# Query and key transposes of a latent-attention layer moved from TensorE to transposing DMAs

## The chip, the cores and the metric

The kernel runs on one core of a Trainium2 chip. The metric is the device time of one execution in microseconds: the median of the runs shown. An engine's work is told by the names of the profile: PE is TensorE, PEld its weight load, DVE VectorE, ACT ScalarE, POOL GpSimd and SP SyncE, which here issues DMAs alone.

## What is computed

Two decoder layers over 512 tokens of width 1024: multi-head latent attention (MLA), then sparse attention (NSA). The change touches only the first:

```python
def mla_mixer(h, pos, w_in, g_cq, w_uq, g_ckv, w_ukv, g_q, g_k, w_out):
    c_q, c_kv, k_pe, z = jnp.split(h @ w_in, [384, 640, 704], axis=-1)
    q = (rms_norm(c_q, g_cq) @ w_uq).reshape(B, S, 16, 192)
    kv = (rms_norm(c_kv, g_ckv) @ w_ukv).reshape(B, S, 16, 128 + 128)
    k_nope, v = kv[..., :128], kv[..., 128:]
    k = jnp.concatenate([broadcast(k_pe), k_nope], axis=-1)      # 64 + 128
    q = rope(rms_norm(q, g_q), pos, 64)
    k = rope(rms_norm(k, g_k), pos, 64)
    o = causal_block_attention(q, k, v, 192 ** -0.5)             # softmax(q k^T) v
    return (o.reshape(B, S, 2048) * silu(z)) @ w_out
```

The inputs are float32. Matmuls that need the precision are made of high and low pieces: a = a_hi + a_lo, and a product is hi x hi + hi x lo + lo x hi (helper `mm3`, lines 97 to 99).

## The kernel before

The attention of layer 0 is a hand-written pipeline over `SLOTS0` = 64 slots: 16 heads times 4 tiles of 128 tokens (slot s is head s // 4, tile i = s % 4). No planner orders it: each engine has a function `step(s)` that writes its instructions of slot s in the order in which they stand, and semaphores tie the engines together. An engine runs its own list strictly in that order. Before slot 0 stand eight slots (`KV0` = -8) with only the early steps.

On PE a slot s is, in order: `scores(s)`, five fp16 matmuls of one query tile with the (i + 1) x 128 keys up to it (lines 97 to 99, 1249, 1250); `turn(s + 4)`; `project_kv(s + 8)`, six matmuls of 256 columns; in slots with i = 1 `values` of the head before (line 1280, eight matmul records); `turn_probs(s - 1)`, transposes of the softmax weights (1263) and of a part of the gate (1270); in even slots `project_q`, nine matmuls of 384 columns, for one tile of a pair of heads.

`turn(m)` (lines 1231, 1232) makes four float32 transposes of 128 x 128 by matmuls with the identity: the 128 plain columns and the doubled 64 rotated columns of the query tile `qn` and of the key tile `kn`, four slots before their scores, into one of two PSUM banks `x_bank` (banks 6 and 7). ACT's `high(m)` (line 1659) rounds the bank to fp16 into `qkT_hi`; DVE's `low(m)` (2300, 2302, 2304) subtracts that from the bank and writes the low pieces.

What comes before `turn`: ACT's `q_stats` (1638) and `kv_stats` (1649, 1653) take sums of squares, and copy keys and values from PSUM to `kv_sb`; POOL's `q_factor` (1966, 1967) and `k_factors_of` (1974 to 1978) make the norm's factors and the rotated key columns; DVE's `scale_q` (2266) and `scale_k` (2291) scale; POOL's `rotate` (1994 to 1997) turns the rotary columns of the query. What comes after: DVE's `maximum(s)` (2313) masks the scores and takes the maximum, ACT's `exponential(s)` (1667) makes the weights, PE's `turn_probs(s)` turns them in the next slot, and ACT's `probs_out` (1674; DVE's 2320 for i = 2) copies them out for `values`. DVE's `gate` (2332) multiplies a finished head with its gate.

Weights of a head (256 KB for keys and values, 576 KB for a pair's queries) come by DMAs from SP's queue (`load_kv` 1010, `load_q` 1001); ACT splits them (1630, 1622), DVE subtracts (2259, 2254). `project_q` has one bank from tile 4 on (bank 4) and waits until the tile before is scaled; `project_kv` has one from tile 8 on (bank 5) and waits until the tile before is copied out.

## Time and profile before

| | us |
|---|---|
| median of 3 runs | 869.14 (868.8 to 869.91) |
| the profiled execution, its time | 868.95 |
| its span | 867.2 |
| PE busy in the span | 848.3 |
| DVE, ACT, POOL busy | 562.8, 502.0, 485.5 |
| layer 0's attention, scores of slot 0 to scores of slot 63 | 146.9 to 362.6 |

The span is the time between the first and the last record of the profile; 1.75 us of the execution lie around it. Busy time of an engine is the union of its instructions; a matmul's duration overlaps the next one's, so what a matmul costs is the distance from its start to the next start.

### The profile page before, as it was taken

To read this page: it belongs to the slowest core of one execution; us is meant where nothing else is said; L and a number is where in the kernel's file an instruction comes from. 1 tells how busy PE (TensorE), PEld (TensorE's weight loads), DVE (VectorE), ACT (ScalarE), POOL (GpSimd) and SP (SyncE) were. 2 spreads that over 40 slices of the span, in tenths; PEclk is the share of its full clock that TensorE was granted. 3 is DMA by queue.
4 is the path that set the end of the run, shared out by engine and by line. 5 is a ranking of instruction groups with operands and counts; after the bars stand their busy time and mean duration, and the time that the engine had idled before them with its cause. 6 is when DMAs were issued, how large, how long until landed. Compare 5 with 4: busy or idle time off the path is not lost.

```text
span 867.2 us, 16773 instructions
## 1 busy us (share of the span) xinstructions
PE 848.3 (98%) x6041; PEld 709.4 (82%) x6041; DVE 562.8 (65%) x1607; ACT 502.0 (58%) x1151; POOL 485.5 (56%) x627
## 2 busy tenths in 40 slices
PE   6999999999999999999999999999999999999998
PEld 6999998888888888778888888778887677777786
DVE  5899988887878787653111113278689688888521
ACT  6456667887877778652134223434443789898610
POOL 2000407876767686343347424366675699999731
PEclk9999999999999999999999999999999999999999
DMA  6433322111111101122227222222233100100011
GB/s 217 131 98 98 98 79 77 39 52 51 43 28 37 53 14 50 49 97 97 96 93 134 93 92 65 80 97 74 79 97 97 50 3 2 51 3 2 2 49 49
DMA packets 39324, 58.93 MB, mean 68 GB/s; under 512 B 8757, under 2 KB 22346, under 8 KB 39242
## 3 DMA queue, kind: packets, MB, share of 16 engines
q1 hardware_dynamic: 39200, 57.85, 21.4%
q8 instruction: 49, 0.80, 0.4%
q14 instruction: 33, 0.27, 0.1%
q10 hardware_dynamic: 42, 0.01, 0.0%
HBM read 55.63 MB, written 2.10 MB: 67 GB/s over the span
## 4 chain that ended last, share of the span: by engine, by line
PE 85%; DVE 8%; ACT 3%; issue 2%; POOL 1%; DMA 0%; ACTq 0%; DVEq 0%; POOLq 0%
PE bank L97 19%; PE bank L99 18%; PE bank L98 18%; PE bank L1280 4%; DVE w_lo L2180 2%; PE bank L502 2%; PE bank L484 2%; PE bank L1263 2%; PE bank L511 2%; PE bank L503 2%; PE bank L1231 1%; PE bank L1232 1%; PE bank L591 1%; PE bank L592 1%; PE bank L590 1%
## 5 line engine op out<-in xcount | busy, mean ns | idle before, releaser
L2003 POOL TENSOR_TENSOR w_lo<-w_raw,w_hi 128x2048 fp32r<-128x2048 f32 (+1 forms) x26 | 118.4, 4554 | 124.0 <-ACT w_hi L1728 123.9
L97 PE MATMUL bank<-w_hi,h_hi 128*128 128x512 f32 (+3 forms) x472 | 171.4, 363 | 1.7 <-DVE h_lo L2100 1.0
L99 PE MATMUL bank<-w_hi,h_lo 128*128 128x512 f32 (+3 forms) x472 | 166.8, 353 | 0.0
L98 PE MATMUL bank<-w_lo,h_hi 128*128 128x512 f32 (+3 forms) x472 | 166.8, 353 | 0.0
L1728 ACT ACTIVATE w_hi<-w_raw 128x2048 fp32r<-128x2048 f32 (+1 forms) x26 | 49.2, 1893 | 94.0 <-PE bank L99 94.0
L97 PEld LDWEIGHTS bank<-w_hi,h_hi 128*128 128x128 f32 x472 | 88.7, 188 | 15.1 <-issue 3.4
L99 PEld LDWEIGHTS bank<-w_hi,h_lo 128*128 128x128 f32 x472 | 88.7, 188 | 11.5
L98 PEld LDWEIGHTS bank<-w_lo,h_hi 128*128 128x128 f32 x472 | 88.9, 188 | 10.1
L789 POOL TENSOR_TENSOR p<-kvr,p 128x512 f16<-128x512 f32 (+1 forms) x96 | 88.5, 942 | 10.1 <-ACT p L705 9.9
L97 PE MATMUL bank<-w_hi,o_hi 128*128 128x512 f32 x192 | 77.2, 402 | 0.8 <-DVE o_lo L2340 0.8
L99 PE MATMUL bank<-w_hi,o_lo 128*128 128x512 f32 x192 | 75.8, 395 | 0.0
L98 PE MATMUL bank<-w_lo,o_hi 128*128 128x512 f32 x192 | 75.8, 395 | 0.0
L97 PE MATMUL bank<-w_hi,c_hi 128*128 128x256 f32 (+1 forms) x224 | 75.6, 337 | 0.0
L98 PE MATMUL bank<-w_lo,c_hi 128*128 128x256 f32 (+1 forms) x224 | 68.3, 305 | 0.0
L99 PE MATMUL bank<-w_hi,c_lo 128*128 128x256 f32 (+1 forms) x224 | 68.3, 305 | 0.0
L702 ACT ACTIVATE kvr<-bank,g_cols 128x512 f32<-128x512 f32 (+1 forms) x96 | 60.6, 632 | 7.5 <-PE bank L518 7.5
L839 DVE CUSTOM_DVE_ANT_0 scored<-bank,band 128x128 f32<-128x128 f32 (+3 forms) x128 | 56.1, 483 | 10.3 <-PE bank L484 10.3
L705 ACT ACTIVATE p<-bank,g_cols 128x512 f16<-128x512 f32 (+1 forms) x96 | 60.8, 633 | 0.0
L2313 DVE CUSTOM_DVE_ANT_0 below<-bank,band,g_cols 128x128 f32<-128x128 f32 (+1 forms) x64 | 34.4, 538 | 23.3 <-PE bank L1250 23.0
L1659 ACT ACTIVATE qkT_hi<-bank 128x512 f16<-128x512 f32 x64 | 38.3, 598 | 12.6 <-PE bank L1232 12.5
L97 PEld LDWEIGHTS bank<-w_hi,o_hi 128*128 128x128 f32 x192 | 36.1, 188 | 9.1 <-POOL w_lo L2003 1.0
L97 PEld LDWEIGHTS bank<-w_hi,c_hi 128*128 128x128 f32 x224 | 42.2, 188 | 1.3
(367 smaller groups left out, 2440.9 us busy)
## 6 DMA issues: line engine op xcount, KB each, us to landing
w_raw<-in_nsa_w_in SPq DMA_DIRECT2D x10, 1024.0 KB, 5.0
w_raw<-in_mla_w_in SPq DMA_DIRECT2D x8, 1024.0 KB, 5.2
w_raw<-in_mla_w_out SPq DMA_DIRECT2D x8, 1024.0 KB, 5.0
w_raw<-in_nsa_w_in SPq DMA_DIRECT2D x8, 984.0 KB, 5.0
w_raw<-in_nsa_w_out SPq DMA_DIRECT2D x4, 1024.0 KB, 5.1
w_raw<-in_mla_w_uq SPq DMA_DIRECT2D x7, 576.0 KB, 4.2
w_raw<-in_mla_w_ukv SPq DMA_DIRECT2D x15, 256.0 KB, 2.7
w_raw<-in_mla_w_in SPq DMA_DIRECT2D x4, 704.0 KB, 5.7
```

Source lines behind the costliest of these rows:

```text
L97: nc.tensor.matmul(out, a[0], b[0], start=start, stop=False)
L98: nc.tensor.matmul(out, a[0], b[1], start=False, stop=False)
L99: return nc.tensor.matmul(out, a[1], b[0], start=False, stop=stop)
L702: nc.scalar.activation(p32(k, u), src, ACT.Exp, scale=score_scale[:, 0:1])
L705: nc.scalar.activation(piece_of(p1, n, u), src, ACT.Exp, scale=score_scale[:, 0:1]).then_inc(exp_done, 1)
L789: nc.gpsimd.tensor_tensor(piece_of(p2, n, u), p32(k, u), piece_of(p1, n, u), ALU.subtract).then_inc(sub_done, 1)
L839: last = nc.vector.tensor_tensor_reduce(scored[k % 2][:, w * keys:(w + 1) * keys], first_bank(k)[:, w * keys:(w + 1) * keys], band[:, SEQ ...
L1280: last = nc.tensor.matmul(o_bank[:, j * P:SEQ], kv_sb[:, h % 4 * NT + j, NOPE:WKV], probT[h % 2][:, j * ROW + j * P:j * ROW + SEQ], start= ...
L1659: nc.scalar.activation(qkT_hi[m // NT % 2][:, :, t * P:(t + 1) * P], x_bank[m % 2][:, :].rearrange("p (a t) -> p a t", a=4), ACT.Copy).the ...
L1728: nc.scalar.activation(w_hi[g % 2][:, :, 0:width], w_raw[g % 2][:, :, 0:width], ACT.Copy).then_inc(m_hi, 1)
L2003: nc.gpsimd.tensor_tensor(w_lo[g % 2][:, :, 0:width], w_raw[g % 2][:, :, 0:width], w_hi[g % 2][:, :, 0:width].bitcast(F32), ALU.subtract). ...
L2313: nc.vector.tensor_tensor_reduce(below[i % 2][:, 0:keys], score_bank[i % 2][:, 0:keys], band[:, SEQ - keys:SEQ], score_scale[:, 1:2], -LEA ...
```

## The change

The turned query and key pieces no longer come from PE. They are made before they are turned, in fp16 in SBUF, and a DMA turns them:

- `turn` on PE, `high` on ACT, `low` and `scale_k` on DVE and the two banks `x_bank` go. The key's gain is multiplied into the query's gain once, so keys need no gain of their own.
- ACT's `key_high(m)` rounds a key tile to fp16 straight from `kv_sb`, three slots behind its projection, and `query_high(m)` a query tile of two heads from `qn`, four slots behind. DVE's `key_low` and `query_low` make the low pieces in the same slots. A key tile then is 4 blocks of 128 fp16 columns (`k16`, three pairs of tiles), a query tile of one head 3 blocks (`q16`, six tiles of two heads).
- SP's new `turn(m)` issues two transposing DMAs from SBUF to SBUF, 3 blocks (96 KB) and 4 blocks (128 KB), into `qkT`. It waits until tile m - 2 has landed whole, so that at most two tiles are in flight, and until the scores of the head two before are done. PE's `scores(s)` waits until both have landed. 64 tiles make 128 such DMAs, 14 MB.
- Weight loads stand among them in SP's queue, four slots earlier in its list than their split. `mid_piece(1)` (1 MB for the next stage) moves from behind the loop to slot 52 of it.
- The freed banks go to the projections: from tile 4 and 8 on `project_q` and `project_kv` alternate between two banks each, and wait for the tile before the last instead of the last.
- POOL writes the rotated columns once, not doubled, and its `k_factors_of(m)` waits until the pair of tiles six and five before has landed.

```diff
+Q32, Q16, KPAIRS = 3, 6, 3
...
+        LATENT_GAINS = SPARSE_GAINS + 1
...
+                k16 = [place(f"k16_{b}", (22, 24, 31)[b] * KB, [P, 2, KCOLS], F16) for b in range(KPAIRS)]
+                qn = place("qn", 26 * KB, [P, Q32, 2, QK])
...
-                qkT_hi = [place(f"qkT_hi{a}", (54 + 8 * a) * KB, [P, 4, SEQ], F16) for a in range(2)]
-                qkT_lo = [place(f"qkT_lo{a}", (70 - 4 * a) * KB, [P, 3, SEQ], F16) for a in range(2)]
-                kn = place("kn", 86 * KB, [P, QRING, WIDE])
+                qkT = [place(f"qkT{a}", (54 + 7 * a) * KB, [P, 7, SEQ], F16) for a in range(2)]
+                q16 = place("q16", 83 * KB, [P, Q16, 2, QCOLS], F16)
                 rot = place("rotq", 92 * KB, [P, 4, 2, HALF0])
...
-                x_bank = [bank[6], bank[7]]
...
-                SLOTS0, KV0, T0 = H * NT, -8, -4
+                SLOTS0, KV0, AHEAD = H * NT, -8, 3
...
-                q_of = lambda m: bank[(4, 0, 3, 2)[m]] if m < NT else bank[4]
-                kv_of = lambda m: bank[1] if m < 2 * NT and m % 2 else bank[5]
+                q_of = lambda m: bank[(4, 0, 3, 2)[m]] if m < NT else bank[4 + m % 2 * 3]
+                kv_of = lambda m: bank[1] if m < 2 * NT and m % 2 else bank[5 + m % 2]
...
-                x_tile = lambda s: s - T0 if 0 <= s - T0 < SLOTS0 else None
+                k_split, q_split = (lambda s: k_tile(s - 3)), (lambda s: q_tile(s - 4))
...
+                all_landed = lambda eng, m: eng.wait_ge(x_landed[m % 2], 32 * (m // 2 + 1))
...
+                    def turn(m):
+
+                        n, t = m // NT, m % NT
+                        mq, tok = n // 2 * NT + t, slice(t * P, (t + 1) * P)
+                        if m >= 2:
+                            all_landed(sp, m - 2)
+                        if n >= 2:
+                            sp.wait_ge(s_done, NT * (n - 1))
+                        sp.wait_ge(x_lo, q_pieces[mq])
+                        sp.dma_start_transpose(qkT[n % 2][:, 0:3, tok], q16[:, mq % Q16, n % 2, :]).then_inc(x_landed[m % 2], 16)
+                        sp.wait_ge(x_lo, k_pieces[m])
+                        sp.dma_start_transpose(qkT[n % 2][:, 3:7, tok], k16_of(m)).then_inc(x_landed[m % 2], 16)
+
...
+                        if s == SLOTS0 - 12:
+                            mid_piece(1)
+                        if 0 <= s + AHEAD < SLOTS0:
+                            turn(s + AHEAD)
+                        if (k_weights(s + 4) or 0) > 1:
+                            load_kv(k_weights(s + 4))
+                        if (q_weights(s + 4) or 0) > 1:
+                            load_q(q_weights(s + 4))
...
-                        if m > NT:
-                            pe.wait_ge(q_scaled, m)
+                        if m == NT + 1:
+                            pe.wait_ge(z_sum, Z_STEPS * NZ)
+                        if m > NT + 1:
+                            pe.wait_ge(q_scaled, m - 1)
...
-                        if 2 <= m <= 2 * NT:
+                        if m >= 2:
                             pe.wait_ge(kv_out, m - 1)
-                        if m > 2 * NT:
-                            pe.wait_ge(kv_out, m)
...
-                    def turn(m):
...
-                        dst = x_bank[m % 2]
-                        q, k = qn[:, mq % QRING, n % 2, :], kn[:, m % QRING, :]
-                        for part, src in enumerate((q, k)):
-                            nc.tensor.transpose(dst[:, 2 * part * P:(2 * part + 1) * P], src[:, 2 * ROPE:WIDE], ident[:, :])
-                            last = nc.tensor.transpose(dst[:, (2 * part + 1) * P:(2 * part + 2) * P],
-                                                       src[:, 0:2 * ROPE], ident[:, :])
-                        last.then_inc(x_done, 1)
...
-                        pe.wait_ge(x_free, s + 1)
+                        all_landed(pe, s)
...
-                        if x_tile(s) is not None:
-                            turn(x_tile(s))
...
-                            act.wait_ge(k_scaled, m - NT + 1)
+                            act.wait_ge(x_lo, k_pieces[m - NT])
...
-                    def high(m):
-                        act.wait_ge(x_done, m + 1)
-                        t = m % NT
-                        nc.scalar.activation(qkT_hi[m // NT % 2][:, :, t * P:(t + 1) * P],
-                                             x_bank[m % 2][:, :].rearrange("p (a t) -> p a t", a=4),
-                                             ACT.Copy).then_inc(x_hi, 1)
+                    def key_high(m):
+
+                        act.wait_ge(kv_out, m + 1)
+                        act.wait_ge(k_rotated, m // 2 + 1)
+                        nc.scalar.activation(k16_of(m)[:, 0:NOPE], kv_sb[:, m % (4 * NT), 0:NOPE], ACT.Copy,
+                                             scale=ms_k[:, m % NT:m % NT + 1]).then_inc(x_hi, 1)
+
+                    def query_high(m):
+
+                        act.wait_ge(q_rotated, m + 1)
+                        if m >= Q16:
+                            all_landed(act, (m - Q16) // NT * 2 * NT + NT + (m - Q16) % NT)
+                        nc.scalar.activation(q16[:, m % Q16, :, ROPE:ROPE + QK], qn[:, m % Q32, :, :], ACT.Copy).then_inc(x_hi, 1)
...
+                        if k_split(s) is not None:
+                            key_high(k_split(s))
+                        if q_split(s) is not None:
+                            query_high(q_split(s))
...
-                        if x_tile(s) is not None:
-                            high(x_tile(s))
...
+                        if m >= 2 * KPAIRS:
+                            all_landed(pool, m - 2 * KPAIRS)
+                            all_landed(pool, m - 2 * KPAIRS + 1)
+                        nc.gpsimd.tensor_tensor(k16[m // 2 % KPAIRS][:, :, 2 * P:3 * P].rearrange("p m (c d) -> p m c d", c=2),
...
+                        nc.gpsimd.tensor_tensor(q[:, :, 0:HALF0], rot[:, 0], rot[:, 3], ALU.subtract)
+                        nc.gpsimd.tensor_tensor(q[:, :, HALF0:ROPE], rot[:, 1], rot[:, 2], ALU.add).then_inc(q_rotated, 1)
...
+                        if m >= Q32:
+                            dve.wait_ge(x_lo, q_pieces[m - Q32])
...
+                    def key_low(m):
+
+                        dve.wait_ge(x_hi, k_pieces[m])
+                        k, factor = k16_of(m), ms_k[:, m % NT:m % NT + 1]
+                        nc.vector.scalar_tensor_tensor(k[:, NOPE:2 * NOPE], kv_sb[:, m % (4 * NT), 0:NOPE], factor,
+                                                       k[:, 0:NOPE], ALU.mult, ALU.subtract)
+                        nc.vector.scalar_tensor_tensor(k[:, KCOLS - ROPE:KCOLS], kpe_sb[:, m % NT, :], factor,
+                                                       k[:, 2 * P:2 * P + ROPE], ALU.mult, ALU.subtract).then_inc(x_lo, 1)
+
+                    def query_low(m):
+
+                        dve.wait_ge(x_hi, q_pieces[m])
+                        q, whole_q = q16[:, m % Q16, :, :], qn[:, m % Q32, :, :]
+                        nc.vector.tensor_tensor(q[:, :, 2 * P:3 * P], whole_q[:, :, ROPE:QK], q[:, :, P:2 * P], ALU.subtract)
+                        nc.vector.tensor_tensor(q[:, :, 0:ROPE], whole_q[:, :, 0:ROPE], q[:, :, ROPE:P],
+                                                ALU.subtract).then_inc(x_lo, 1)
...
+                            og.link(nc.vector.tensor_tensor(gq0[:, ROPE:QK], gq0[:, ROPE:QK], gk0[:, ROPE:QK], ALU.mult))
```

How PE's list changes, in slot 3 of head 0 (i = 3): the last two of the scores, then what follows. Before:

```order
L1249 MATMUL bank<-qkT_hi_99 128x512
L1250 MATMUL bank<-qkT_lo_101,qkT_hi_99 128x512
L1231 MATMUL bank<-ident,qn 128x128
L1232 MATMUL bank<-ident,qn 128x128
L1231 MATMUL bank<-ident,kn 128x128
L1232 MATMUL bank<-ident,kn 128x128
L97 MATMUL bank<-w_hi,c_hi 128x256
L98 MATMUL bank<-w_lo,c_hi 128x256
L99 MATMUL bank<-w_hi,c_lo 128x256
```

Now:

```order
L1255 MATMUL bank<-qkT_102 128x512
L1256 MATMUL bank<-qkT_102 128x512
L97 MATMUL bank<-w_hi,c_hi 128x256
L98 MATMUL bank<-w_lo,c_hi 128x256
L99 MATMUL bank<-w_hi,c_lo 128x256
```

The four transposes are gone and the projection stands right behind the scores. The same goes in all 64 places where `turn` stood, slots -4 to 59.

ACT's list, from the exponential of slot 2 (384 keys) through that of slot 3 (512 keys). Before:

```order
L1667 ACTIVATE prob,rowsum<-below_106,negmax 128x384
L1638 ACTIVATE sq_junk,ms_q<-bank 128x192 x2
L1659 ACTIVATE qkT_hi_100<-bank 128x4x128
L1649 ACTIVATE sq_junk,ms_k<-bank 128x128
L1653 ACTIVATE kv_sb<-bank,ms_c 128x256
L1667 ACTIVATE prob,rowsum<-below_107,negmax 128x512
L1659 ACTIVATE qkT_hi_99<-bank 128x4x128
```

Now (`k_1_72` is a `k16`, `q_104` is `q16`):

```order
L1678 ACTIVATE prob,rowsum<-below_107,negmax 128x384
L1664 ACTIVATE k_1_72<-kv_sb,ms_k 128x128
L1642 ACTIVATE sq_junk,ms_q<-bank 128x192 x2
L1653 ACTIVATE sq_junk,ms_k<-bank 128x128
L1657 ACTIVATE kv_sb<-bank,ms_c 128x256
L1678 ACTIVATE prob,rowsum<-below_108,negmax 128x512
L1664 ACTIVATE k_1_72<-kv_sb,ms_k 128x128
L1672 ACTIVATE q_104<-qn 128x2x192
```

The rounding of the turned bank stood between `q_stats` and `kv_stats`, behind PE's transposes; now a smaller one of the keys stands at the slot's start, in even slots followed by that of the queries.

SP's list around one load of a pair's query weights. Before there was nothing but loads (three here, two of them the same); now:

```order
L1074 DMA_TRANSPOSE qkT_102<-q_104 128x3x128
L1076 DMA_TRANSPOSE qkT_102<-k_1_72 128x4x128
L1009 DMA w_raw<-in_mla_w_uq 128x3x384
L1074 DMA_TRANSPOSE qkT_103<-q_104 128x3x128
L1076 DMA_TRANSPOSE qkT_103<-k_2_73 128x4x128
L1074 DMA_TRANSPOSE qkT_103<-q_104 128x3x128
L1076 DMA_TRANSPOSE qkT_103<-k_2_73 128x4x128
L1018 DMA w_raw<-in_mla_w_ukv 128x2x256
```

Between two weight loads now lie two or four tiles, each with two transposing DMAs that wait for pieces of their slots.

## Rows read from the trace of the kernel before

**Rows 1.** The page, part 1: busy time of each engine
```profile
PE 848.3 (98%) x6041; PEld 709.4 (82%) x6041; DVE 562.8 (65%) x1607; ACT 502.0 (58%) x1151; POOL 485.5 (56%) x627
```

**Rows 2.** The page, part 4: shares of the chain that ended last
```profile
PE 85%; DVE 8%; ACT 3%; issue 2%; POOL 1%; DMA 0%; ACTq 0%; DVEq 0%; POOLq 0%
```

**Rows 3.** Busy us by stretch: total, then PE, PEld, DVE, ACT, POOL, PEclk, DMA, GB/s
```profile
157.44:341.78 184.34, 184.34 (x1292) 157.36 (x1292) 146.20 (x460) 144.22 (x496) 136.61 (x288) 1.00 0.13 40
139.87:157.44 17.57, 15.52 (x116) 14.20 (x115) 14.43 (x48) 15.38 (x53) 14.00 (x31) 1.00 0.16 49
```

**Rows 4.** Timeline, PE: start us, us, engine, line, operation, out<-in, count
```profile
244.33 0.27 PE L1231 MATMUL bank<-ident,qn 128*128 128x128 f32 x1
...
244.69 0.37 PE L97 MATMUL bank<-w_hi,c_hi 128*128 128x256 f32 x1
...
246.09 0.28 PE L1231 MATMUL bank<-ident,qn 128*128 128x128 f32 x1
246.20 0.27 PE L1232 MATMUL bank<-ident,qn 128*128 128x128 f32 x1
...
246.42 0.27 PE L1232 MATMUL bank<-ident,kn 128*128 128x128 f32 x1
246.56 0.36 PE L97 MATMUL bank<-w_hi,c_hi 128*128 128x256 f32 x1
...
247.35 0.60 PE L1263 MATMUL bank<-ident,prob 128*128 128x128 f32 x4
```

**Rows 5.** Timeline, ACT, the same two slots
```profile
245.68 0.28 ACT L1649 ACTIVATE sq_junk<-bank 128x128 f32<-128x128 f32 x1
...
246.31 0.72 ACT L1667 ACTIVATE prob<-below,negmax 128x512 f32<-128x512 f32 x1
246.92 0.20 ACT L1667 ACTIVATION_READ_ACCUMULATOR prob<-below,negmax 128x1 f32 x1
```

**Rows 6.** Groups by line and shape, 157.44 to 341.78 us: busy us, mean ns
```profile
L1659 ACT ACTIVATE qkT_hi<-bank 128x512 f16<-128x512 f32 x52 | 31.2, 599 | 11.4 <-PE bank L1232 11.3
...
L2291 DVE SCALAR_TENSOR_TENSOR kn<-kv_sb,ms_k,gk 128x128 f32<-128x128 f32 x52 | 23.3, 449 | 0.0
...
L2300 DVE TENSOR_TENSOR qkT_lo<-bank,qkT_hi 128x256 f16<-128x256 f32 x52 | 21.6, 415 | 0.5 <-ACT qkT_hi L1659 0.5
...
L2302 DVE TENSOR_TENSOR qkT_hi<-bank,qkT_hi 64x128 f16<-64x128 f32 x52 | 15.3, 294 | 0.7
...
L2304 DVE TENSOR_TENSOR qkT_lo<-bank,qkT_hi 64x128 f16<-64x128 f32 x52 | 14.7, 282 | 0.7
...
L1685 ACT ACTIVATE zT<-bank 128x256 f32<-128x256 f32 x25 | 9.7, 386 | 0.1
...
L1674 ACT ACTIVATE probT<-bank 128x128 f32<-128x128 f32 x13 | 3.6, 278 | 22.7 <-PE bank L1270 22.7
```

**Rows 7.** DMA issues: line, queue, count, KB each, us to landing
```profile
w_raw<-in_mla_w_ukv SPq DMA_DIRECT2D x15, 256.0 KB, 2.7
...
v_diag<-vcmp SPq DMA_DIRECT2D x4, 32.0 KB, 4.1
```

**Rows 8.** Timeline, SP: four issues of 32 KB
```profile
604.35 2.64 SPq L1079 DMA_DIRECT2D v_diag<-vcmp  x4
```

**Rows 9.** Timeline, PE, the first slots: two waits on the subtraction
```profile
143.03 0.30 PE L1231 MATMUL bank<-ident,qn 128*128 128x128 f32 x1 [0.70 <-DVE qkT_lo L2304]
...
148.74 0.30 PE L1231 MATMUL bank<-ident,qn 128*128 128x128 f32 x1 [1.35 <-DVE qkT_lo L2304]
```

**Rows 10.** Timeline, POOL, the first slots
```profile
143.62 0.50 POOL L1994 TENSOR_TENSOR rotq<-qn,tcos 128x128 f32<-128x128 f32 x1 [1.70 <-DVE qn L2266]
...
146.90 0.61 POOL L1978 TENSOR_TENSOR kn<-kpe_sb,ms_k 128x256 f32<-128x256 f32 x1
```

**Rows 11.** Timeline, PE, slot 56: its wait on the exponential
```profile
345.69 0.66 PE L1263 MATMUL bank<-ident,prob 128*128 128x128 f32 x4 [0.48 <-ACT prob L1667]
```

More of the change, by code:

```diff
@@ L2347, in step @@
                             z_sums(NB - 1)
[L2348 to L2349 removed]
+                        if k_split(s) is not None:
+                            key_low(k_split(s))
                         if 1 <= s <= SLOTS0 and s % NT == 3:
                             probs_out(s - 1)
[L2352 to L2353 removed]
+                        if q_split(s) is not None:
+                            query_low(q_split(s))
                         if q_tile(s - 1) is not None:
```

107 lines of the change are left out of this document (36 added, 71 removed).

## The prediction

> **What bounds the kernel now.** I read the page's first part before anything else: PE is busy 848.3 of 867.2 us [rows 1], and it holds 85% of the chain that ended last [rows 2]. So a change of PE's list moves the end, and one of another engine does so only where PE comes to wait for it. Then busy time by stretch. From 157.44 us (the scores of slot 3) to 341.78 us (those of slot 55) lie 13 groups of four slots, and PE is busy in all of the 184.34 us at a granted clock of 1.00 [rows 3]: 14.18 us a group, 3.545 us a slot. The others are busy in that stretch, over 13: DVE 11.2, ACT 11.1, POOL 10.5 us a group. There the whole of what PE sheds is gain, until one of them ends later than PE. In the first slots (139.87 to 157.44) PE is busy 15.52 of 17.57 us, so about 2 us of waits lie there.
>
> The timeline of PE shows one seam closely [rows 4]. `turn` takes 0.44 us: its four transposes start 0.11 apart, from 246.09 to 246.42, so it ends at 246.53.  The 273 ns of one transpose overlap the next and are not the price.
>
> **What PE sheds.** 64 x 0.44 = 28.2 us. That is the upper bound of the gain of this part, and 52 of the 64 lie in the steady stretch, 4 x 0.44 = 1.76 us a group.
>
> **What comes to be late next.** The walk through one group [rows 4, 5] looks for the wait that takes the place. Of PE's waits on ACT the closest is `turn_probs` of i = 3. The last projection of slot 3 starts at 244.69; ACT's `kv_stats` begins when it is through, at 245.68, the exponential of 512 keys begins at 246.31 and its read ends at 247.12. Its transposes start on PE at 247.35. So 0.23 us stand between the two. In that interval PE loses just one `turn`, that of slot 0 (the one of slot 3 lies ahead of the projection and shifts both). PE then is ready at 247.35 - 0.44 = 246.91, and ACT, which still begins `kv_stats` behind the same projection, at 247.12 plus some 0.05: PE waits 0.26, say 0.29 us. That is once a group. In the other three slots PE has a query projection or `values` between the turns of the weights; the same walk leaves some 0.3 us to spare for i = 1, and more for the rest. Two-bank projections cost nothing and give nothing here: PE has no wait on a projection's bank in the steady stretch, and none can be won. They are needed as PE comes sooner, and they hide ACT's copies.
>
> Steady stretch: 13 x (1.76 - 0.29) = 19.1 us; a slot then takes 12.71 / 4 = 3.18 us.
>
> **The other engines.** ACT loses 4 x 0.60 and gains four key roundings of 128 columns and two query roundings of 384 columns a group. Nearest rows: 0.28 for 128 columns, 0.39 for 256, 0.60 for 512 [rows 6], so 4 x 0.28 + 2 x 0.49 = 2.1, and ACT stands at 10.8 of 12.7 us. None of the new ones waits for PE: their slot is three or four behind. DVE loses 4 x (0.45 + 0.42 + 0.29 + 0.28) = 5.8 us and gains 4 x (0.45 + 0.29) + 2 x (0.42 + 0.29) = 4.4 [rows 6]: 9.8 us. POOL writes half as much in two of a rotation's four instructions and stays under its 10.5. All three fit into 12.7, so I cost them at nothing beyond the 0.29. If that cover is gone (an engine at 100%), each microsecond of its group is paid 13 times.
>
> **The transposing DMAs.** The trace has none, and this is the open price. Per tile there are two, of 96 and 128 KB. From below: a plain load of 256 KB lands 2.7 us after its issue; from above: a copy from SBUF to SBUF of 32 KB lands in 4.1 us [rows 7]. SP needs 2.64 us for four such issues [rows 8], 0.66 each, so its queue can issue a tile in 1.3 us if a transposing issue costs no more. Two bounds count. Rate: a tile must pass in 3.18 us. At 2.7 us each DMA it passes in 2.7 if a tile's two run one behind the other and two tiles overlap, in 1.4 if all four overlap. Delay: the tightest tile is i = 3 of an even head. Its query pieces are made in slot 4n and its scores stand three slots later, 9.5 us; by the walk the pieces are through some 3.5 us into the slot, so 6 us remain. Two DMAs one behind the other at 2.7 land in 5.4. I take both as hidden, by the row nearer in size; at 4.1 each, 8.2 us, they would be about 2 us late once in eight slots.
>
> Here one page of the Trainium skill speaks against the change and one for it. By the Trainium skill, VectorE: DVE Perf Modes, "The three transpose paths", a DMA transpose of 128x128 bf16 takes 1309 ns, against 390 ns on TensorE; if that held per block, seven blocks made 9.2 us a tile, an estimate, and the sum would turn from -21 to some +340 us. By the Trainium skill, Advanced Engine Details and Errata, "X-Bar Transpose (TRN2)", transposing DMAs are about as fast as plain ones (350-400 GB/s); 224 KB would then pass in some 0.6 us, an estimate, and the sum stays. No row here shows either.
>
> **The two ends.** First slots: eight turns, 3.5 us, and two waits of PE on the subtraction for the bank, 0.70 and 1.35 us [rows 9], could all go: 5.5 us at most. But POOL is the slow one there: a rotation and a pair of key factors run from 143.62 to 147.51 [rows 10], and now ACT, in its own order, cannot pass the key rounding that needs them. Walking the lists, the first turned weights come some 3 us sooner and those of slot 1 only 2. At least nothing; I take 2.0. Last slots: slot 56 waits 0.48 us for its exponential already [rows 11], so the turns of slots 56 to 59 were free, and I count 0.4 for slot 55's. `mid_piece(1)` in another place is not waited for and costs nothing.
>
> **The sum.** 19.1 + 2.0 + 0.4 = 21.5 us. The profiled execution took 868.95 us (its span 867.2), so 847.4; the median stands 0.2 above that, and I predict **847.6 us**.
>
> **Rivals.**
> First, the other sign: **the transposing DMAs pass more slowly than the slots**. One mechanism: SP waits until tile m - 2 has landed, PE until its own has, and from then on a slot lasts as long as a tile's two DMAs. It decides from 3.18 us a tile on; from 3.545 us on the change loses. Over 60 slots: at 4.1 us a tile, (4.1 - 3.545) x 60 = +33, about 902; at 2.7 us for each of the two with no overlap, 5.4: +111, about 980; at 4.1 each, 8.2: +279, about 1148. For it: the copy that stays in SBUF is the slow row, 4.1 us for an eighth of the bytes [rows 7], and a queue that serves turned blocks one at a time fits both ends. Against it: the DMA engines' share is 0.13 in the stretch [rows 3], and that copy touches 32 partitions. The 1309 ns of the Trainium skill, told above, would be this rival at its far end. 0.25.
> Second, **the pieces come late, not slowly**: landings of 6 to 8 us from the piece, or POOL and ACT held in their queues by the new waits on landings, so that PE waits 0.3 to 1.2 us more a group: 13 x 0.3 to 13 x 1.2, 4 to 16 us given back, 852 to 864. POOL has 2.2 us a group to spare, and DVE now has two SBUF sources in more of its instructions. 0.14.
> Third, **the gain is eaten whole**: the weights' loads stand behind waiting turns and come late, or the waits above sum to 20 us; within 0.2% of before. 0.04.
> Fourth, above my forecast: the wait of 0.29 does not come and the first slots give all: 28 us, about 841. It is inside the forecast's own spread.
>
> **The numbers.** Forecast 0.57, its own range 841 to 852. All that I call unknown is the DMA, so the chances follow from it. Faster by over 0.2% (about what a measurement of this kernel can tell from no change): 0.57 + 0.14 = 0.71. Same 0.04. Slower 0.25, of which about a quarter lies below 885 us. The range is 842 to 885: it leaves out some 0.01 below and 0.19 above.
>
> **What would show it.** In the profile after: no matmul from `ident` and `qn` or `kn`, and the projection 0.22 us behind the last start of the scores; a group of four slots of 12.7 us; before `turn_probs` of i = 3 a wait of about 0.3 us on ACT's exponential, 14 or so times; ACT over 80% busy there; no wait of PE on the first score matmul. A transposing DMA landing in 2 to 3 us and SP waiting for pieces, not for landings. The prediction is wrong if the score matmuls wait for DMAs in every slot (the first rival: then a slot's length is that of two landings), or if they wait once in eight slots (the second).

## The result and the profile after

The changed kernel takes **854.76 us** (median of 4 runs, 853.98 to 856.51), the kernel before beside it 869.52: a ratio of 0.9833, 95% interval 0.9814 to 0.9852. That is 14.8 us faster, where I had forecast 21.5: outside the forecast's own 841 to 852 us, inside the range of 842 to 885. The profiled execution took 855.4 us, its span 853.6. Of the four executions two, this one and that of 856.51 us, have a mean granted clock of TensorE of 0.994, and two (854.13 and 853.98 us) one of 0.998.

The page of the changed kernel, part 1 and the shares of the chain that ended last:

```profile
PE 827.9 (97%) x5785; PEld 686.6 (80%) x5785; DVE 552.8 (65%) x1544; ACT 493.1 (58%) x1183; POOL 484.2 (57%) x628
...
PE 79%; DVE 9%; ACT 5%; issue 3%; DMA 2%; SPq 1%; POOL 1%; ACTq 0%; DVEq 0%; POOLq 0%
```

PE lost 20.4 us of busy time against [rows 1], the span only 13.6: about 7 us became idle time of PE, and its share of the chain fell from 85% to 79% [rows 2]. To see where, I cut both spans at the same five instructions: the first matmul of the query projection of tile 3 (slot -5, the second projection behind the z products), the first score matmul of slots 3, 55 and 63, and the end.

| stretch | before, us | after, us | difference | forecast |
|---|---|---|---|---|
| start to tile 3's query projection | 138.29 | 139.50 | +1.21 | 0 |
| to the scores of slot 3 | 19.15 | 19.54 | +0.39 | -2.0 |
| to the scores of slot 55 (13 groups) | 184.34 | 166.26 | -18.08 | -19.1 |
| to the scores of slot 63 | 20.81 | 23.78 | +2.97 | -0.4 |
| to the end of the span | 504.61 | 504.52 | -0.09 | 0 |
| sum | 867.2 | 853.6 | -13.60 | -21.5 |

The steady stretch did what it should. Most of what is missing lies in its two ends. Busy us of the changed kernel in the three middle stretches (total, then PE, PEld, DVE, ACT, POOL, granted clock, DMA share, GB/s), to be read beside [rows 3] and beside the same two end stretches of the kernel before, which come first:

```profile
138.29:157.44 19.15, 17.09 (x126) 15.75 (x125) 15.98 (x52) 16.12 (x56) 14.78 (x33) 1.00 0.14 45
341.78:362.59 20.81, 19.38 (x124) 14.42 (x122) 15.75 (x52) 15.89 (x42) 9.11 (x10) 1.00 0.15 52
```
```profile
139.50:159.04 19.54, 16.77 (x98) 15.07 (x97) 15.25 (x49) 16.23 (x60) 14.03 (x33) 0.83 0.42 94
159.04:325.30 166.26, 163.81 (x1084) 135.93 (x1084) 135.33 (x407) 136.82 (x522) 134.68 (x284) 1.00 0.57 117
325.30:349.08 23.78, 19.30 (x104) 13.16 (x102) 17.51 (x44) 14.78 (x42) 11.03 (x14) 0.93 0.47 107
```

The granted clock was 1.00 in all of this before; now it is 0.83 and 0.93 in the ends. PE is idle in them for 2.77 and 4.48 us (before 2.06 and 1.43). In the steady stretch, DVE, ACT and POOL are busy for 81 to 82% (10.4, 10.5, 10.4 us a group of 12.8).

**The steady stretch.** The seam that [rows 4] and [rows 5] showed before, on PE and on ACT of the changed kernel (timeline: start us, us, engine, line, operation):

```profile
201.09 0.28 PE L99 MATMUL bank<-w_hi,c_lo 128*128 128x256 f32 x1
201.51 0.65 PE L1269 MATMUL bank<-ident,prob 128*128 128x128 f32 x4
```
```profile
200.02 0.28 ACT L1653 ACTIVATE sq_junk<-bank 128x128 f32<-128x128 f32 x1 [0.43 <-PE bank L99]
...
200.29 0.47 ACT L1657 ACTIVATE kv_sb<-bank,ms_c 128x256 f32<-128x256 f32 x1
200.65 0.72 ACT L1678 ACTIVATE prob<-below,negmax 128x512 f32<-128x512 f32 x1
201.26 0.20 ACT L1678 ACTIVATION_READ_ACCUMULATOR prob<-below,negmax 128x1 f32 x1
```

Products of 256 columns start 0.12 us apart, so PE would have begun the turn of the weights at 201.21; it began at 201.51, 0.05 behind the exponential's read. This is the wait of 0.29 us once a group. PEld's group of the same line has idled 3.8 us for the exponential, 0.29 on the mean of the 13 groups (the waits stand in 11 of them, at most 0.4 each):

```profile
L1269 PEld LDWEIGHTS bank<-ident,prob 128*128 128x128 f32 x130 | 15.1, 140 | 3.8 <-ACT prob L1678 3.8
L97 PE MATMUL bank<-qkT 128*128 128x512 f16 (+3 forms) x52 | 15.9, 305 | 0.9 <-DMA qkT<-k 0.9
```

The second row is the other loss: PE waits twice for a landing, together 0.9 us, at 187.63 and 265.04. A group of four slots took 14.30 us before and takes 12.87 now, two of them 13.23 and 13.04. The last of the 13 has less work in either kernel: 12.71 us before, 11.28 now.

**The transposing DMAs.** SyncE's timeline, and the view of all instructions on `qkT` (duration in ns, min/median/max, then the time from issue to landing):

```profile
204.28 1.18 SPq L1074 DMA_TRANSPOSE qkT<-q  x1
205.50 1.26 SPq L1076 DMA_TRANSPOSE qkT<-k  x1
206.81 0.58 SPq L1009 DMA_DIRECT2D w_raw<-in_mla_w_uq  x1
```
```profile
L1074 SPq DMA_TRANSPOSE qkT<-q x64: 1177/1190/2217, 143.9 to 342.3; - x64
L1076 SPq DMA_TRANSPOSE qkT<-k x64: 1249/1264/2268, 145.2 to 343.6; - x64
...
DMA to landing us min/median/max: 2.3/2.5/5.6
```

They land in 2.5 us in the median, the queries' 96 KB and the keys' 128 KB alike, near the 2.7 us that I took. But an issue takes 1.19 and 1.26 us of SP's queue, where I had 0.66: 2.5 us of each slot's 3.2, and a weight load more in some slots. From one tile's first issue to the next tile's it is 2.6 us where SP waits for nothing. By the Trainium skill, VectorE: DVE Perf Modes, "The three transpose paths", a 128x128 block takes 1309 ns; three blocks and four land in the same median of 2.5 us here, so that figure does not add up by blocks. By Advanced Engine Details and Errata of the Trainium skill, "X-Bar Transpose (TRN2)", transposing DMAs run at about the speed of plain ones; the trace agrees (a plain load of 256 KB lands in 2.9 us), but the time to issue does not follow from it.

**The first slots.** PE ends the last projection ahead of slot 0 at 146.05 and then stands. Its timeline, and busy us by stretch (columns as above):

```profile
148.49 0.29 PE L97 MATMUL bank<-qkT 128*128 128x128 f16 x1 [2.44 <-DMA qkT<-k]
```
```profile
146.00:148.50 2.50, 0.06 (x2) 0.01 (x1) 1.67 (x6) 2.19 (x8) 2.19 (x6) 0.89 0.46 95
148.50:151.00 2.50, 2.28 (x12) 2.02 (x13) 1.93 (x5) 2.09 (x10) 0.82 (x3) 0.50 0.43 83
```

Tile 0's query pieces are through at 143.85, its DMAs are issued at 143.88 and 145.22, and the keys have landed at 148.4. The granted clock is 0.50 (1.2 of 2.4 GHz) from 147.95, still in the idle time, until 154.8. What this fall costs can be read from runs told below, whose lists are the same up to slot 3. From the scores of slot 0 to those of slot 3, in the changed kernel, in e1 and in e5 (columns as above):

```profile
148.49:159.04 10.55, 10.33 (x54) 9.03 (x55) 7.29 (x24) 7.91 (x33) 7.92 (x19) 0.70 0.63 142
```
```profile
148.31:157.79 9.48, 9.02 (x55) 8.16 (x55) 6.40 (x22) 7.79 (x33) 7.09 (x18) 0.82 0.56 120
```
```profile
148.09:157.22 9.13, 7.97 (x55) 6.77 (x55) 6.24 (x21) 7.69 (x33) 6.74 (x17) 1.00 0.54 107
```

PE idled 2.44, 2.45 and 2.51 us ahead of them, and yet the clock was at 0.50 for 6.8 us in the first, for 3.4 us in the second and not at all in the third. The long fall costs 1.4 us here against none. A mean clock of 0.998 over the run leaves room for one fall of 3.4 us alone (an estimate, 1.7 of 853.6 us, and the last slots have such a fall); so two of the four executions above probably had no long fall.

**The last slots.** Timelines of DVE, POOL and PE:

```profile
332.56 4.42 DVE L2309 SCALAR_TENSOR_TENSOR k<-kv_sb,ms_k,k 128x128 f16<-128x128 f32 x1 [1.05 <-ACT k L1664]
...
337.17 0.59 DVE L2328 CUSTOM_DVE_ANT_0 below<-bank,band,g_cols 128x384 f32<-128x384 f32 x1
```
```profile
332.31 4.52 POOL L2018 TENSOR_TENSOR w_lo<-w_raw,w_hi 128x2048 fp32r<-128x2048 f32 x1 [0.50 <-ACT w_hi L1741]
```
```profile
338.57 0.55 PE L1269 MATMUL bank<-ident,prob 128*128 128x128 f32 x3 [2.42 <-ACT prob L1678]
```

`key_low` (L2309), 0.35 us elsewhere, took 4.42 and ended 0.15 us behind POOL's first `mid_low`, a subtract of 128x2048 that begins in slot 57. The maximum of slot 58 stands behind it on DVE, ACT's exponential behind that, and PE waits 2.42 us; the clock is 0.50 from 339.1 to 342.5. In the kernel before, the same subtract (349.35, 4.54 us) met subtractions that read a bank of PSUM, and none took long. By the Trainium skill, SBUF — State Buffer, "SBUF: two separate sides", VectorE with two inputs in SBUF and GpSimd share one port pair, which the first holds for its whole instruction; the rows agree.

### The profile page after: what moved, and what is told of

Same layout as the page of the kernel before. It is cut to its first block, busy times and chain, and to the rows that moved or that the text cites. A ratio compares the mean times of both kernels' runs of the same rounds, so it can differ in the third digit from the quotient of the medians.

```text
span 853.6 us, 16381 instructions
## 1 busy us (share of the span) xinstructions
PE 827.9 (97%) x5785; PEld 686.6 (80%) x5785; DVE 552.8 (65%) x1544; ACT 493.1 (58%) x1183; POOL 484.2 (57%) x628
## 4 chain that ended last, share of the span: by engine, by line
PE 79%; DVE 9%; ACT 5%; issue 3%; DMA 2%; SPq 1%; POOL 1%; ACTq 0%; DVEq 0%; POOLq 0%
PE bank L97 18%; PE bank L99 18%; PE bank L98 18%; PE bank L1286 3%; DVE w_lo L2198 2%; PE bank L510 2%; PE bank L492 2%; PE bank L519 2%; PE bank L511 2%; PE bank L1269 1%; DMA qkT<-k 1%; PE bank L599 1%; ACT prob L1678 1%; PE bank L600 1%; PE bank L598 1%
## 5 line engine op out<-in xcount | busy, mean ns | idle before, releaser
L97 PE MATMUL bank<-w_hi,c_hi 128*128 128x256 f32 (+1 forms) x224 | 78.6, 351 | 0.3 <-DVE w_lo L2277 0.2
L98 PEld LDWEIGHTS bank<-w_lo,c_hi 128*128 128x128 f32 x224 | 43.1, 192 | 0.4
```

The source lines that it names most:

```text
L97: nc.tensor.matmul(out, a[0], b[0], start=start, stop=False)
L98: nc.tensor.matmul(out, a[0], b[1], start=False, stop=False)
```

## The experiments

Each kernel was timed beside runs of the kernel before; I compare the ratios, since those runs are not the same for all.

**e1, e2, e3: the two ends.** e1 cuts the subtract:

```diff
-    nc.gpsimd.tensor_tensor(w_lo[g % 2][:, :, 0:width], ...)
+    for k, c in parts:          # g == 0: KP x 2 parts of 128x256; else one
+        last = nc.gpsimd.tensor_tensor(w_lo[g % 2][:, ks, cs], ...)
+    last.then_inc(m_lo, 1)
```

> The changed kernel with GpSimd's first mid_low (128x2048 subtract, 4.52 us) cut into eight subtracts of 128x256, about 0.57 us each by size. Theory A (GpSimd's long subtract holds VectorE's key_low, which has two operands in SBUF, for 4.42 us in place of 0.35, and all of the tail's loss follows from that): key_low takes at most about 1 us here, the idle time of TensorE before the turned probabilities of slot 58 falls from 2.42 to under 0.5 us, the 3.4 us at a granted clock of 0.50 behind it go, the last group of slots takes 11 to 12 us in place of 14.18, and the kernel 851.5 to 852.5 us against the changed kernel's 854.8. Rival B (VectorE is held until GpSimd's whole row of subtracts is done, whatever their size): the last group stays near 14.2 us, 854.8. Rival C (the clock falls there for another reason): the wait goes, the clock still falls, some 853.

Measured: 852.26 us (852.05 to 853.73), ratio 0.9813 (0.9799 to 0.9826). By the ratios that is 1.7 us less than the changed kernel, and the two intervals overlap a little; the cleaner pair is e2 and e3 below, timed together and apart by this edit alone. The timelines of DVE and of PE in e1:

```profile
331.94 0.63 DVE L2314 SCALAR_TENSOR_TENSOR k<-kv_sb,ms_k,k 128x128 f16<-128x128 f32 x1 [1.12 <-ACT k L1664]
```
```profile
334.98 0.39 PE L97 MATMUL bank<-qkT 128*128 128x512 f16 x1 [0.96 <-DMA qkT<-k]
...
337.59 0.23 PE L97 MATMUL bank<-qkT 128*128 128x128 f16 x1 [1.02 <-DMA qkT<-k]
```

`key_low` is held for about one eighth of the subtract, 0.6 to 0.9 us; the wait for the exponential and the fall of the clock are gone, and slots 55 to 63 take 21.22 us in place of 23.78. Theory A holds and B and C fall. In place of the old wait PE now waits twice, about 1 us each, for the DMAs of slots 59 and 60: these two slots take 2.61 and 2.60 us, and SP begins a tile every 2.6 us there (333.81, 336.42, 339.02).

e2 makes the first query pieces earlier:

```diff
-k_split, q_split = (lambda s: k_tile(s - 3)), (lambda s: q_tile(s - 4))
+k_split, q_split = (lambda s: k_tile(s - 3)), (lambda s: q_tile(s - 3) if s < KV0 + 6
+                    else None if s == KV0 + 6 else q_tile(s - 4))
```

> The changed kernel with the query pieces of tiles 0 to 2 made one slot earlier (slots -5 to -3 in place of -4 to -2). Theory A (TensorE's 2.44 us of waiting before the scores of slot 0 come from tile 0's queries being made last, and the 6.8 us at a granted clock of 0.50 behind it come from that idle time): query pieces of tile 0 are ready near 140.5 instead of 143.85, the wait goes, the clock stays at 1.00, slot 3 begins 3 to 5 us earlier, and the kernel takes 850 to 852 us. Rival B (slot 3 is set by the other engines: GpSimd's factors and the weights' split are late anyway): the wait at slot 0 goes but turns up before slots 1 to 3, slot 3 begins under 1 us earlier, 854 to 855. Rival C (the transposing DMAs of tile 0 are slow for another reason, such as the weights' load beside them): the wait at slot 0 stays over 1 us.

Measured: 854.68 us (854.09 to 855.42), ratio 0.9837 (0.9824 to 0.9851): nothing won, as rival B has it. PE's waits in e2's timeline, and its stretch behind slot 0:

```profile
148.07 0.39 PE L97 MATMUL bank<-w_hi,c_hi 128*128 128x256 f32 x1 [2.21 <-DVE w_lo L2277]
151.84 0.27 PE L97 MATMUL bank<-qkT 128*128 128x256 f16 x1 [1.21 <-ACT kv_sb L1657]
153.76 0.33 PE L1269 MATMUL bank<-ident,prob 128*128 128x128 f32 x1 [0.50 <-ACT prob L1678]
156.55 0.44 PE L1269 MATMUL bank<-ident,prob 128*128 128x128 f32 x2 [0.94 <-ACT prob L1678]
```
```profile
148.50:151.00 2.50, 2.14 (x14) 1.82 (x12) 0.92 (x4) 1.36 (x7) 0.97 (x2) 1.00 0.54 144
```

The scores of slot 0 begin 6.41 us after tile 3's query projection instead of 8.99, with no wait, and the clock stays at 1.00. But PE then waits 2.21 us for the split of head 2's weights and another 2.65 us for ACT, and slot 3 begins 19.42 us after the projection against 19.54.

e3, both edits:

> Both edits of the two runs before. Theory: the two losses are 200 us apart and add up: 847 to 850 us, near the 847.6 forecast. Rival: one of them is eaten elsewhere (a wait at the end of the latent stage that takes whatever comes early), and the sum is no better than the better of the two by itself.

Measured: 852.25 us (851.95 to 852.42), ratio 0.9808 (0.9795 to 0.9822), the same as e1. The rival holds, and e2's edit is worth nothing in the time. Against e2 the subtract in eighths is worth 2.4 us, and no execution of the one reaches those of the other.

In the first slots e3's trace has the same lists as e2's, and takes 18.35 us where that took 19.42. The first step apart is GpSimd's `rotate`; e2, then e3:

```profile
144.70 1.16 POOL L2009 TENSOR_TENSOR rotq<-qn,tcos 128x128 f32<-128x128 f32 x1 [1.60 <-DVE qn L2286]
```
```profile
144.76 0.46 POOL L2009 TENSOR_TENSOR rotq<-qn,tcos 128x128 f32<-128x128 f32 x1 [1.60 <-DVE qn L2291]
```

Beside it run DVE's subtractions with two inputs in SBUF. In e2 they run on and POOL takes longer; in e3 two of them take longer (0.51 and 0.70 instead of 0.28 and 0.42 us). So e2's 19.42 is no limit. Without the edit the stretch takes 19.54 with the long fall of the clock, 18.49 with the short one (e1) and 18.20 with none (e5); with it 18.35. Where the clock holds, the other engines set slot 3 and the edit gives nothing; only against the long fall is it 1.2 us shorter.

**e4: what PE's turns are worth.** The kernel before, with `turn`'s loop run twice:

```diff
-for part, src in enumerate((q, k)):
+for part, src in ((0, q), (1, k)) * 2:
```

> The kernel before with each tile's four TensorE transposes made twice into the same bank: 0.44 us more TensorE work a tile, nothing more on any other engine. Theory (TensorE sets the slots of the kernel before, so its work counts one for one): +0.44 x 52 = 22.9 us in the steady stretch, and 24 to 28 in all: 893 to 898 us. Rival (a part of the transposes lies in time in which TensorE waits anyway, 0.1 to 0.2 us a tile): +13 to +20, 883 to 890.

Measured: 892.09 us, ratio 1.0269 (1.0255 to 1.0283), 23.2 us over the kernel before it, 0.9 below the theory's range and 2 above the rival's. The groups take 15.94 us instead of 14.30: 1.64 of the 1.76 us are passed on. So PE's work counts nearly one for one, and the first slots, where seven turns (slots -4 to 2) add 3.1 us, took only 1.4 us more (20.54 instead of 19.15).

**e5: the wait on the exponential.** On the kernel of e1:

```diff
+if 0 <= s < SLOTS0 and s % NT == 3:
+    exponential(s)
 if k_tile(s):
     kv_stats(k_tile(s))
...
-if 0 <= s < SLOTS0:
+if 0 <= s < SLOTS0 and s % NT != 3:
     exponential(s)
```

> The kernel of e1 (852.3 us) with ScalarE's exponential of every slot with i = 3 ahead of the slot's statistics of the key-value projection instead of behind them. Theory (the 0.29 us a group that I took as a new wait is real and is this: TensorE has finished the projection and waits for the exponential, which stands behind two instructions that waited for the projection): a group takes 12.57 to 12.60 in place of 12.87 us, 13 x 0.28 = 3.6 us, and the kernel 848.5 to 849.5 us. Rival (the key and value rows leave their bank 0.8 us later and something else, the next key's pieces or their transposing DMA, takes the wait over): groups of 12.8 to 13.1, no gain.

Measured: 850.51 us (849.35 to 851.47), ratio 0.9785 (0.9772 to 0.9799), 2.4 us less than e1 by the ratios and above the theory's 848.5 to 849.5. The same seam on PE and PEld's group over the stretch:

```profile
200.38 0.28 PE L99 MATMUL bank<-w_hi,c_lo 128*128 128x256 f32 x1
200.50 0.60 PE L1269 MATMUL bank<-ident,prob 128*128 128x128 f32 x4
```
```profile
L1269 PEld LDWEIGHTS bank<-ident,prob 128*128 128x128 f32 x133 | 15.6, 140 | 0.4 <-ACT prob L1678 0.4
L97 PE MATMUL bank<-qkT 128*128 128x128 f16 (+3 forms) x52 | 15.9, 306 | 3.0 <-DMA qkT<-k 3.0
```

The turn now follows 0.12 us behind the projection, and the undisturbed groups take 12.51 us, 0.36 less. But waits for landings rise to 3.0 us (1.0 in e1), and some groups take up to 13.98, so slot 3 to slot 55 is only 1.1 us shorter than in e1. The theory on the wait holds; a good part of what it gives goes to the next one, the landings.

**e6: the multiply of the gains.** The key gains are folded into the query gains by one instruction on DVE, which I had not priced. On the kernel of e1:

```diff
-        og.link(nc.vector.tensor_tensor(gq0[:, ROPE:QK], gq0[:, ROPE:QK], gk0[:, ROPE:QK], ALU.mult))
...
 split_q(1)
+og.link(nc.vector.tensor_tensor(gq0[:, ROPE:QK], gq0[:, ROPE:QK], gk0[:, ROPE:QK], ALU.mult))
 nc.vector.memset(rinv[:, :, :], 1.0).then_inc(o_free, 1)
```

> The kernel of e1 (852.3 us) with the added multiply of the query gains by the key gains (VectorE, 0.29 us at 99.47) moved out of the z products' stage to just ahead of the first slot. Theory (it lies in VectorE's chain, on which TensorE waits there; the stretch from 97 to 106 us took 8.46 us in place of 8.16): 0.3 us less, 851.9 to 852.1, which only the trace can tell. Rival (VectorE has slack there and the 0.3 us have another origin): the stretch still takes 8.46.

Measured: 851.68 us, ratio 0.9798 (0.9785 to 0.9811), not to be told from e1 by the time. The row of the changed kernel on DVE:

```profile
99.47 0.29 DVE L2398 TENSOR_TENSOR gq<-gq,gk 128x128 f32<-128x128 f32 x1
```

Between the same two products of the z stage PE takes 8.16 us before, 8.46 after the change, and 8.16 in e6. So 0.3 of the 1.21 us ahead of the slots is this instruction.

**e7: one bank each.** The changed kernel with the banks and waits of before:

```diff
-q_of = lambda m: bank[(4, 0, 3, 2)[m]] if m < NT else bank[4 + m % 2 * 3]
-kv_of = lambda m: bank[1] if m < 2 * NT and m % 2 else bank[5 + m % 2]
+q_of = lambda m: bank[(4, 0, 3, 2)[m]] if m < NT else bank[4]
+kv_of = lambda m: bank[1] if m < 2 * NT and m % 2 else bank[5]
...
-if m > NT + 1:
-    pe.wait_ge(q_scaled, m - 1)
+if m > NT:
+    pe.wait_ge(q_scaled, m)
...
-if m >= 2:
-    pe.wait_ge(kv_out, m - 1)
+if 2 <= m <= 2 * NT:
+    pe.wait_ge(kv_out, m - 1)
+if m > 2 * NT:
+    pe.wait_ge(kv_out, m)
```

> The changed kernel with one bank for the query projections and one for the key-value projections in the steady slots, as before the change, and the waits that go with it. Theory (with TensorE at 12.6 of 12.9 us a group and ScalarE emptying a bank 0.8 us after its projection, a projection finds its bank free a slot later anyway): within 1 us of 854.8, groups of 12.87. Rival (the second bank carries part of the gain, since without the turn there is 0.44 us less between a bank's last product and its next first): groups 0.3 to 1 us longer, 859 to 868.

Measured: 858.23 us (857.94 to 860.04), ratio 0.9879 (0.9866 to 0.9893), 4.0 us more than the changed kernel by the ratios, between the theory and the rival. What PE waited for from 145 to 350 us (line, releaser, total, times, longest):

```profile
PE bank L97 <- DMA qkT<-k: 3.9, 4, 2.4
PE bank L97 <- ACT kv_sb L1659: 3.7, 12, 0.3
PE bank L1271 <- ACT prob L1680: 3.5, 3, 2.3
PE bank L97 <- DVE qn L2288: 1.9, 1, 1.9
```

A new wait of 0.3 us comes once a group, but the group grows by only 0.12 us (12.99), as it covers part of the next wait: 1.6 us in 13 groups. The first slots grow by 2.2 us (21.75 instead of 19.54), where a query projection waits 1.9 us for its bank, and the last ones by 0.9, where the clock is at 0.50 for 6.9 us in place of 3.4. The second banks carry about 4 us of the gain, part of it through the clock. My "give nothing" holds only for the kernel before; "needed as PE comes sooner" is what the run shows.

**e8: the margin of the DMAs.** One tile in flight:

```diff
-if m >= 2:
-    all_landed(sp, m - 2)
+if m >= 1:
+    all_landed(sp, m - 1)
```

> The changed kernel with SyncE waiting for the landing of tile m - 1 instead of m - 2 before it issues tile m: one tile's two transposing DMAs in flight. Theory (a tile's period is then two issues of 1.2 and 1.26 us and the landing of the second, 2.5 us after its issue began, so about 3.8 us, and 5.0 if the 2.5 count from its end): TensorE waits for landings in every slot, groups of 15.2 to 20 us, the kernel 880 to 950: the rival of my prediction that the DMAs pass slower than the slots, and its deciding point of 3.2 us. Rival (landings overlap the next tile's issue even so): under 860.

Measured: 904.33 us, ratio 1.0404 (1.039 to 1.0418). SyncE's timeline in e8, and PE's waits from 150 to 400 us:

```profile
215.31 1.19 SPq L1074 DMA_TRANSPOSE qkT<-q  x1
216.54 1.26 SPq L1076 DMA_TRANSPOSE qkT<-k  x1
219.04 1.18 SPq L1074 DMA_TRANSPOSE qkT<-q  x1
```
```profile
PE bank L97 <- DMA qkT<-k: 45.9, 39, 2.9
```

A tile's period is 3.73 us, one issue and one landing, and the groups take 15.1 to 16.8. This is the first rival of the prediction, made real: at 3.73 us a tile, 0.2 over its second bound of 3.545, the kernel loses 35 us to the one before. Its point of decision was right; the formula (60 x the excess, 11 us) was too low. The 52 steady slots took 4.00 us each, not 3.73, 23.6 us in all over the kernel before: SP also issues the weights' loads in this queue, and some issues took up to 2.4 us. Another 9.9 us came in the last eight slots, which took 2.6 us each before. What keeps the change on the good side is that the next tile's issues overlap the landings.

**e9, e10, e11, e12: what is left.** e9 puts the edits of e1, e2, e5 and e6 together.

> The four edits together: GpSimd's subtract in eighths (e1), the exponential first where i = 3 (e5), the multiply of the gains moved (e6), the first three tiles' query pieces a slot earlier (e2). Theory (e5 showed that SyncE's queue with two issues of 1.2 and 1.26 us a tile, and the landings behind it, is what ends waits now, so that an earlier slot 3 and shorter groups are given back there): 849.5 to 850.5 us, with TensorE's waits for landings at the slots near 187, 212 and 288 us again. Rival (the gains add up: 0.3 for the multiply, 0.4 for the earlier start): 849.0 to 849.5.

Measured: 850.33 us (849.13 to 851.58), ratio 0.9785 (0.9773 to 0.9798), as e5 and in the theory's range. The waits for landings are there again. SP's timeline behind a load of 576 KB, and PE's:

```profile
180.25 0.57 SPq L1009 DMA_DIRECT2D w_raw<-in_mla_w_uq  x1
180.95 3.11 SPq L1074 DMA_TRANSPOSE qkT<-q  x1
```
```profile
187.26 0.23 PE L97 MATMUL bank<-qkT 128*128 128x128 f16 x1 [1.75 <-DMA qkT<-k]
```

e10 cuts this load in thirds (`part` is a third), one a slot; e11 issues each of them two slots earlier:

```diff
-if (q_weights(s + 4) or 0) > 1:
-    load_q(q_weights(s + 4))
+for part in range(KQ):
+    if (q_weights(s + 6 - part) or 0) > 1:        # e10: s + 4 - part
+        load_q(q_weights(s + 6 - part), part)
```

> The kernel of e9 with each load of query weights for a pair of heads (576 KB, one in eight slots, directly ahead of a tile's transposing DMAs) cut into three loads of 192 KB, one in each of three slots. Theory (in e5 TensorE's waits for landings, 0.25 to 1.31 us, stand at 160, 187, 212 and 288 us, each behind such a load, on whose packets the transposing DMAs wait in the 16 engines): those waits shrink to under 0.3 us, 1.5 to 2 us less than e9. Rival (it is SyncE's time to issue, which three loads of 0.5 us only lengthen): the same as e9 or up to 2 us slower.

Measured: 863.03 us (860.08 to 864.77), ratio 0.9932 (0.9917 to 0.9946). PE has no wait for a landing in the steady stretch but one of 0.5 us at its end; ACT, however, has one for the last third, which is issued two slots later than the whole load was, and all that stands behind it on ACT waits too. ACT's timeline:

```profile
191.77 1.16 ACT L1628 ACTIVATE w_hi<-w_raw 128x1152 fp32r<-128x1152 f32 x1 [2.32 <-DMA w_raw<-in_mla_w_uq]
```

Behind it comes the copy of the turned weights, for which PE waits 11.4 us in five places. I had overlooked that wait; neither the theory nor the rival has it.

> The kernel of e10 with each third loaded two slots earlier, so that the last of them is issued where the whole load was in e9. In e10 TensorE's waits for landings were gone from the steady stretch, but ScalarE waited for the last third (TensorE idle 1.6 to 3.3 us at each second head behind it). Theory (landings behind the 576 KB load were the whole of what e9 loses against groups of 12.51): all groups near 12.5, 13 of them 163.5 us in place of e9's 166.9, and the kernel 846.5 to 848 us. Rival (three issues of 0.5 us more in SyncE's queue and a third's packets still ahead of a tile's make the tiles late in smaller portions): 849 to 851.

Measured: **848.11 us** (847.18 to 848.23), ratio 0.9759 (0.9746 to 0.9773), 2.3 us less than e9 and the fastest version, 0.1 over the theory's range. Of PE's groups from slot 3 to 55 none waits for a landing but the last, 0.59 us; they take 12.50 and 12.70 us in turn (one 13.21, one 13.59, the last 11.68), 164.29 us in all against 166.95 in e9. So the landings behind the large load were most of what e9 lost against 12.5 a group.

e12 changes both ends once more:

```diff
+k_splits = lambda s: 2 if s == -3 else None if s == -2 else k_weights(s)   # ACT and DVE
...
-if s == SLOTS0 - 8:
+if s == SLOTS0 - 9:
     mid_high(0)
...
-if s == SLOTS0 - 7:
-    mid_low(0)
+if s in (SLOTS0 - 8, SLOTS0 - 7, SLOTS0 - 6):
+    mid_low(0, (slice(0, 3), slice(3, 6), slice(6, 8))[s - SLOTS0 + 8])
```

> The kernel of e11 with two more edits. (1) The split of head 2's key and value weights on ScalarE and VectorE one slot earlier, at slot -3, ahead of ScalarE's 1.28 us of table load: TensorE's 2.2 us of waiting for it at 148 us goes; theory: slot 3 begins 0.5 to 1.5 us earlier, the rest comes back as waits for ScalarE and the pair's key pieces; rival: nothing, as in e2. (2) ScalarE's rounding for the output product at slot 55 instead of 56 and GpSimd's eighths over slots 56 to 58 (3, 3, 2): TensorE's 0.6 to 0.9 us of waiting for them at slot 60 goes. Together 0.5 to 2 us under e11; if both rivals hold, the same as e11.

Measured: 851.97 us (850.29 to 853.89), ratio 0.9807 (0.9793 to 0.9822), 4 us slower than e11, which neither theory had. Its ACT and PE timelines in slots 55 and 56:

```profile
325.68 1.90 ACT L1746 ACTIVATE w_hi<-w_raw 128x2048 fp32r<-128x2048 f32 x1
```
```profile
328.82 4.11 PE L1289 MATMUL bank<-probT,kv_sb 128*128 128x512 f32 x8 [2.10 <-ACT probT L1688]
```

The rounding, a slot earlier, stands on ACT ahead of the copy of the turned weights, for which PE waits 2.10 us before `values`; its eight products then take 4.11 us instead of 2.42, with the clock at 0.50 from 329.35 to 332.8. Slots 55 to 63 take 23.45 us against 21.15 in e11. The first slots gave nothing either (18.59 us to slot 3 against 18.36). Of the 4.0 us between the two spans another 1.3 lie in the start, ahead of both edits.

## Why the prediction was right in kind and 7 us too high in the gain

**Right.** PE bounds and what it sheds counts (e4: 1.64 of 1.76 us a group). The steady stretch saved 18.08 us of 19.1 forecast. The wait that takes the place is the one named, of the size named (0.30 at the seam, 0.29 by PEld's group), and goes when the order on ACT is changed (e5). Landings take 2.5 us where I took 2.7, SP waits for pieces more than for landings, and ACT is at 82% of the steady stretch. Of the remaining 1.0 us the two groups with late landings hold 0.5; the rest is that an undisturbed group became 1.43 us shorter, not 1.47. That the kernel got faster at all rests on this stretch.

**"The two ends", last slots: -0.4 forecast, +2.97 measured.** This is the largest miss. I had written that DVE now has two SBUF sources in more of its instructions, but only as a point for the second rival's price a group, and never asked which long GpSimd instruction runs beside them: `mid_low` at slot 57, 4.5 us, was in the trace of before. e1 shows the cause: in eighths, 2.6 us come back. Of the rest, PE's waits of e1 for landings, with a tile of SP every 2.6 us, are the likely cause; no run changes them alone.

**First slots: -2.0 forecast, +0.39 measured.** The part took eight turns for the seven that stand there, which changes nothing in the 2.0. I counted a saving of turned weights coming sooner and named POOL as the gate, but left out that tile 0's DMAs add 4.6 us from the pieces made in slot -4 (143.85) to the landing (148.44), and gave the clock no term. With the clock held, the changed lists save 0.95 us (18.20 in e5 against 19.15); with the short fall 0.66 (e1); the long fall, in the profiled execution and in e6 (19.64), turns that into a loss. e3 (18.35) shows that without the wait for the landing nothing more is won, as the weights' split and ACT take over. So the step that failed is the 2.0: it was twice what the orders give, and the clock can take the rest. This also means that about 1 us of the 3.2 us between e1's profile and the changed kernel's is the shorter fall and not e1's edit. What stays open is why the same idle time of PE brings a long fall, a short one or none.

**Start: 0 forecast, +1.21 measured.** 0.3 us is the multiply that I did not price (e6). The other 0.9 is there by the 24th us, ahead of all that the change touches, and comes and goes from kernel to kernel: the 92nd matmul starts at 23.08 us before, at 22.55 in e4, which has all of the old code, at 23.99 after, and from 22.64 (e6) to 24.50 (e10) in changed kernels. I can put it to nothing in the change, and its cause stays open.

**The transposing DMAs: "0.66 each, if a transposing issue costs no more".** It costs 1.19 and 1.26 us. That SP's queue was still fast enough, 2.5 against 3.2 us a slot, kept the error small in the steady stretch (PE waits 0.9 us), but the last slots of e1 wait for it. That e5 gave 2.4 and not 3.6 us (1.1 in the steady stretch itself) lies more in the loads of 576 KB ahead in the queue, as e11 shows. The second rival's times, 852 to 864, held the result; its mechanism, pieces late in each group, did not: both large losses stand once each. That the time fell where that rival put it is luck.

## What to carry to other kernels

Where a change gives an engine instructions with two inputs in SBUF, list the long GpSimd instructions of the whole program and ask which of them now meets one; cut the long one in pieces. Price a DMA three times over, in the time to issue it on its queue, in its landing and in what it queues behind, and do it for the shortest slots, not for the mean one. When PE sheds work, the stretches where it was the bound give nearly all of it; where it already waited, the first slots here, 3.1 us of turns gave 0.95 us at best.
